# A cap of four gathers in flight on GpSimd, in a two-block network kernel on one Trainium2 core

## What is computed

```python
def block(xc):                      # 128 tokens
    q = (xc @ wq).reshape(C, 8, 2, 128)
    s = jnp.einsum('chpd,hpnd->chpn', q, sub_keys)
    ...                             # two top-16 searches, then top-16 of their sums
    g = jax.nn.softmax(top, axis=-1)
    a = jax.nn.gelu(jnp.einsum('chkd,cd->chk', u_tab[eidx], xc))
    return jnp.einsum('chk,chkd->cd', g * a, v_tab[eidx])
```

## Time and profile before

| | |
|---|---|
| median of 3 runs | 3764.98 us |
| lowest, highest | 3761.07, 3767.07 us |
| span of the profiled execution | 3950.5 us |
| first gather issued, last row used | 462.0 us, about 3144 us |
| DMA engines, mean over the span | 274 GB/s |
| mean granted TensorE clock | 0.858 of full speed |

### The profile page before, as it was taken

The page is one execution under the profiler, slowest core; times in us unless marked ns, Lnnn a source line. Parts: engine busy times, 40 slices in busy tenths (PEclk is TensorE's granted clock), DMA queues, the critical chain, the costliest instruction groups (busy, mean ns, idle before and its releaser), DMA issues. The chain is left out here.

```text
span 3950.5 us, 31621 instructions
## 1 busy us (share of the span) xinstructions
PE 2885.6 (73%) x8765; PEld 1482.5 (38%) x8765; DVE 2517.4 (64%) x5630; ACT 798.8 (20%) x2049; POOL 1678.8 (42%) x1721
## 2 busy tenths in 40 slices
PE   7998774768778685750487864477528799999998
PEld 3555632214542232220123552222312265566555
DVE  2665877787895778778654388577865534433442
ACT  2243200212222101200123320022002203310331
POOL 1333565665556655656663336366646500000000
PEclk9989887986999897975797975698669999999999
DMA  7544599999999999989995459899999932233222
GB/s 254 173 131 171 202 403 390 337 353 322 396 350 368 358 402 380 347 294 373 358 360 185 163 217 380 326 346 347 383 350 364 336 131 95 86 128 130 96 86 80
DMA packets 349801, 1081.30 MB, mean 274 GB/s; under 512 B 32368, under 2 KB 38972, under 8 KB 348860
## 3 DMA queue, kind: packets, MB, share of 16 engines
q0 software_dynamic: 232064, 847.35, 56.9%
q1 hardware_dynamic: 117564, 231.92, 16.7%
HBM read 1073.92 MB, written 5.24 MB: 273 GB/s over the span
## 5 line engine op out<-in xcount | busy, mean ns | idle before, releaser
L2121 PE MATMUL psum<-lent,heads 128*128 128x512 f32 x616 | 358.8, 683 | 191.3 <-issue 82.2
L2071 DVE SCALAR_TENSOR_TENSOR lent<-lent,psum 128x1024 f32<-128x1024 f32 x308 | 363.2, 1218 | 137.5 <-ACTq L459 109.3
L2105 ACT ACTIVATE heads<-common,dots 128x128 f32<-128x128 f32 x768 | 281.1, 396 | 810.1 <-PE psum L2121 402.9
L2174 POOL DMA_INDIRECT lent<-in_peer_u_dram,picks_u x308 | 289.4, 939 | 279.8 <-DVE lent L2071 180.4
L1162 PE MATMUL psum<-ring,turned 128*128 128x512 f32 (+2 forms) x864 | 351.2, 561 | 57.1 <-issue 42.3
L2174 POOL DMA_INDIRECT lent<-in_peer_v_dram,picks_u x308 | 293.0, 951 | 187.4 <-PE psum L2121 73.6
L2079 DVE SCALAR_TENSOR_TENSOR psum<-lent,dots,psum 128x512 f32<-128x512 f32 x306 | 230.9, 754 | 123.9 <-DMA lent<-in_peer_v_dram,picks_u 82.1
L1166 PE MATMUL psum<-turned,ring 128*128 128x256 f32 x768 | 217.0, 429 | 111.5 <-issue 87.5
L2121 PE MATMUL psum<-turned,heads 128*128 128x512 f32 x304 | 172.0, 659 | 169.0 <-DVE proj L2071 133.4
L2121 PEld LDWEIGHTS psum<-lent,heads 128*128 128x128 f32 x616 | 105.4, 203 | 441.2 <-DMA lent<-in_peer_v_dram,picks_u 272.3
L1608 PE MATMUL psum<-ring,turned 128*128 128x512 f32 x512 | 238.3, 625 | 37.9 <-DMA ring<-in_w_in_dram 9.9
(11 more groups left out here) (348 smaller groups left out, 5174.1 us busy)
## 6 DMA issues: line engine op xcount, KB each, us to landing
ring<-in_w_in_dram SPq DMA_DIRECT2D x35, 2048.0 KB
lent<-in_w_in_dram SPq DMA_DIRECT2D x11, 2048.0 KB, 7.8
proj<-in_ada_w_dram POOLq DMA_DIRECT2D x20, 1024.0 KB, 5.7
heads<-in_ada_w_dram POOLq DMA_DIRECT2D x20, 1024.0 KB, 5.9
ring<-in_w_out_dram SPq DMA_DIRECT2D x8, 2048.0 KB
ring<-in_peer_wq_dram SPq DMA_DIRECT2D x8, 2048.0 KB
lent<-in_w_out_dram SPq DMA_DIRECT2D x6, 2048.0 KB, 9.1
lent<-in_peer_wq_dram SPq DMA_DIRECT2D x4, 2048.0 KB, 9.0
```

Source lines behind the costliest of these rows:

```text
L2071: dve.scalar_tensor_tensor(out=src, in0=src, scalar=1.0, in1=kept_row, op0=ALU.mult, op1=ALU.mult, accum_out=weight).then_inc(rows_used.se ...
L2105: act.activation(diags[n % DIAGS], ident, ACT.Copy, scale=dots[:, j:j + 1]).then_inc(diag_ready.sem, 1)
L2121: pe.matmul(kept_row[:, 0:512], diags[n % DIAGS], row_slot(r)[:, 0:512], start=j == 0, stop=j == PICKS - 1).then_inc(pe_rows.sem, 1)
L2174: pool.indirect_dma_start(out=row_slot(r), out_offset=None, in_=tables_dram[which], in_offset=bass.IndirectOffsetOnAxis(ap=picks_u[:, t, j ...
```

## The change

POOL waits, before it issues gather r, until gather r-4 has landed. It waits on the semaphore of that gather's slot for the count that its landing gives. The wait stands last, just ahead of the issue, and holds for all stages, since r counts through all of them. Nothing else changes.

```diff
     EARLY, LATE = PICKS - 16, 16
     BEHIND = 3
+    IN_FLIGHT = 4
     WEIGH = 8
@@
             if row < ROWS and r % ROWS == ROWS - 1:
                 pool.wait_ge(kept.sem, picked0 + 1)
+            if r >= IN_FLIGHT:
+                pool.wait_ge(gathered[(r - IN_FLIGHT) % ROWS].sem, 16 * ((r - IN_FLIGHT) // ROWS + 1))
             pool.indirect_dma_start(
                 out=row_slot(r), out_offset=None, in_=tables_dram[which],
```

## The result

The changed kernel takes 4182.85 us (median of 4 runs, 4177.52 to 4193.28), the kernel before, timed beside it, 3766.03 us (3761.07 to 3778.84). The ratio is 1.1104 with a 95% interval of [1.1084, 1.1124]: 417 us slower, more than four times the 95 us forecast, and outside the range.

The account below looks back on a forecast made before the run. Bound: DMA in v stretches; in u stretches DMA where weight loads share it, otherwise VectorE. 61 + 31 + 8 = 100 us on the profiled 3950.5, scaled to 95 on the median 3764.98: 3860 us, range 3757 to 3991.

Parts of the forecast that it names:

- What bounds the kernel: In the twelve gather stretches: v bound by DMA, u by DMA where weight loads share the engines, otherwise by VectorE.
- The wait as an instruction: On POOL, before each issue: the added third wait is hidden behind the previous issue's work, 0 us, at most 0.30.
- The wait as a gate: POOL's issues: four gathers share latency 5.38 plus wake-up 0.27 us, so 1.41 us a gather, 0.16 more than now.
- v stretches: Six stretches of 128 v gathers: 20.5 us more each, half absorbed in POOL's pauses, 10 us each charged, 61 in all.
- u stretches: Six stretches of 128 u gathers: first and fifth pay 31 us together, the other four 2 us each, 8.
- The scaling to the median: Whole kernel: 100 us on the profiled span of 3950.5 us, scaled to 95 us on the median of 3764.98.
- rival A: Gathers: four are enough, latency falls to 4.44 us, pace stays 1.25 us, nothing moves; 3765 us, chance 0.16.
- D: POOL's added wait never binds, since slots free later than n-4 lands; time as rival A's, chance within its 0.16.
- B: v stretches: POOL's run-ahead causes its pauses and the gate removes them; 105 us gained, 3665 us, pace below 1.39, chance 0.09.
- C: v stretches: TensorE idles more, its clock falls, half the rows cost 1.71 us; 115 us more, 3970 us, chance 0.13.

Follow-up runs that it names:

- the cap of nine: Changed kernel with IN_FLIGHT 9 in place of 4, so gather n waits for the landing of n-9: 3969.69 us, ratio 1.0013 to the kernel before.
- five and six: Changed kernel with IN_FLIGHT 5 or 6 in place of 4; at the slower level 3962.71 and 3965.48 us, in another set 3959.32 and 3965.88.

## Why the prediction was wrong

*What bounds the kernel* was right at the faster level (DMA share 1.00 in the eighth stretch); at that of the profile it was read from, POOL's pauses stood beside the DMA (0.95). Consumers waiting for landings and a gate that turns the bound into a round trip came out as forecast, and so did the direction.

*The wait as an instruction, 0 us*: right, by the cap of nine (1.0013). But the step asked only what a met wait costs, and not what the place of the wait does to the wake-up where it blocks.

*The wait as a gate, 1.41 us a gather*: this is the term that was mis-sized. It measured 1.64. The wake-up was taken as 0.27 us from the earlier trace rows, where the wait is inside the gather; the added wait is not, and took 0.76 from the start of VectorE's row (0.79 from the landing), worth 0.12 us a gather. The latency was taken as 5.38, the second of four rows, on the argument that a slower issue shortens it; it was 5.66, worth 0.07. That is the mean of the four rows, which the prediction used for the top of its range, by coincidence, since nothing argued for the mean. Together 1.61 of the 1.64 measured.

*v stretches, +61 us*: found +233. Two errors meet. At 1.64 in place of 1.41 the term is more than doubled; and half of it was written off against pauses that the timed executions hardly had. At 1.64 the 768 v gathers owe 0.39 us each, 300 us: at the faster level 233 of it was paid, at the slower one 123. So pauses do absorb, as the prediction said, and more than half where they exist. At the slower level the changed kernel lost 223 us in all (4189.04 - 3966.3), and at the faster 417, with almost the same end time. So some 200 us of the 417 are time that the kernel before is spared at the faster level. The sum of 100 was made for the slower one and was short there in both kinds of stretch: by the profiles, 123 in v for 61, and 109 in u for 39. The mis-sized pace is enough to make up that part; no run takes it apart further.

*u stretches, +39 us*: found +183. Weight loads did cover part, as forecast: the first stretch, with its 14.68 MB of loads, grew by 27 us, the seventh, without any, by 38. The first and the fifth, charged in full with 31 us, grew by 57; the four charged with 2 us each grew by 126. The seventh was expected to have spare time, at 201 us with 180 of gathers at the new pace. At the faster level it took 180 us and then 218.

*The scaling to the median*: this is where the 200 us were lost. The prediction set a profiled execution of 3950.5 us beside a median of 3764.98 and called the 185.5 us a scale. It was another level of the kernel's time, with other pauses on POOL, and neither a factor nor the profiler. The same gap was read once more in rival A, as a hint that latencies might be shorter.

The rivals: A and D did not come; by the landing records 1444 of 1536 gathers were issued as the fourth in flight. B was right in part: the pauses with a free slot and without a consumer are real, and the gate at four removes most of them (43 and 41 to 8 at the slower level). But at a pace of 1.64 us, above the 1.39 that B set as its limit, that gains nothing, and five and six leave the slower level where it is, within 0.3%. C did not come: the granted clock in the eighth stretch is 0.93, against 0.96, far above the 0.8 that C asked. The rule of the Trainium skill ("DMA: Bandwidth & Descriptors", section on the anatomy of one DMA on the gpsimd path) would have made four ample, by its estimate of 4.1 us a gather with POOL's work. The measured latencies of 5.2 to 5.9 us with three to four under way decide against using it for a stream at full rate.

## What to carry to other kernels

A cap on transfers in flight is a closed loop, so its pace is (latency under load + wake-up) / number, and both have to be read where that loop would run: latency with the queue filled, wake-up for a wait in the place where the new one will stand. A wait that may block belongs first, next to its instruction in the traces here; one that is always met can stand anywhere. And when a profiled execution lies 5% from the timed median, the two are to be explained before one is used to price the other.

## What was unexpected of the hardware

- The same wait took 0.76 us from the start of VectorE's row to POOL's issue when written last, and 0.24 us when written first (0.79 and 0.26 from the landing).
- The kernel before has two levels 5% apart (3765 and 3965 us) that hold for a whole set of runs, with pauses of about 3 us on POOL at the same gathers at the slower one. The changed kernel takes 4183 and 4189 us at the two, and has few of the pauses at either.
- Latency from issue to landing rises from 5.2 us with three gathers in flight to 6.9 with six and 10.1 without a cap, while the pace stops improving at about 1.3 us.
